# Band scores in row halves, five early gates, and a new order in the even steps of a hybrid attention layer

## The reference, cut to what matters

```python
h  = rms_norm(x, mix_norm)
c_q, c_kv, k_pe, q_s, k_s, v_s = split(h @ w_in)
y_mla = mla_attention(c_q, c_kv, k_pe, ...) @ w_o_mla      # 8 heads, block-causal
y_swa = swa_attention(q_s, k_s, v_s, rel_bias, sinks) @ w_o_swa
g_mla, g_swa = sigmoid(h @ w_gate)                         # 2 x 1024 columns: 16 tiles of 128
x = x + (g_mla * y_mla + g_swa * y_swa) @ w_out

# swa_attention: 8 chunks of 64 queries, 16 query heads, 2 key heads of width 64,
# each chunk sees its own 64 keys and the 64 before it (the "band" of 128 keys)
logits = einsum('bcqhgd,bckhd->bchgqk', q, kb) * 64 ** -0.5 + rel_bias
m = maximum(max(logits), sink)
p = exp(logits - m);  p = p / (sum(p) + exp(sink - m))
o = einsum('bchgqk,bckhd->bcqhgd', p, vb)
```

## Time and profile before

| | |
|---|---|
| median of 3 runs | 1121.86 us (1121.82 to 1121.98) |
| the profiled execution, its own time | 1122.17 us |
| its span | 1120.4 us |
| mean granted TensorE clock | 0.998 |
| busy in the span: PE, DVE, ACT, POOL | 1109.7, 567.0, 419.0, 149.1 us |

### The profile page before, as it was taken

One profiled execution on the slowest core, in us unless ns is written; L12 is line 12 of the kernel. 1 busy time (PEld: TensorE's weight loads), 2 busy tenths in 40 slices (PEclk: granted clock), 3 DMA queues, 4 the chain that ended last, 5 costly groups with the idle time before them and its releaser, 6 DMA issues.

```text
span 1120.4 us, 14760 instructions
## 1 busy us (share of the span) xinstructions
PE 1109.7 (99%) x5194; PEld 908.4 (81%) x5194; DVE 567.0 (51%) x852; ACT 419.0 (37%) x719; POOL 149.1 (13%) x119
## 2 busy tenths in 40 slices
PE   9999999999999999999999999999999999999996
PEld 7888888888888888777777788888888888888896
DVE  6644344433455536876565554546443444434454
ACT  7322222222335325776544533334221233212253
POOL 0211011100114102320000002231110011101122
PEclk9999999999999999999999999999999999999999
DMA  7235222332224221051321232322233222323222
GB/s 269 87 100 122 95 94 94 97 105 98 94 70 132 98 94 61 11 149 50 118 72 62 73 97 94 95 94 94 94 98 105 97 94 94 94 95 103 88 71 76
DMA packets 35262, 107.21 MB, mean 96 GB/s; under 512 B 4224, under 2 KB 7968, under 8 KB 35216
## 3 DMA queue, kind: packets, MB, share of 16 engines
q1 hardware_dynamic: 34464, 105.43, 29.1%
q0 software_dynamic: 192, 0.78, 0.6%
q10 hardware_dynamic: 560, 0.41, 0.1%
HBM read 101.76 MB, written 2.88 MB: 93 GB/s over the span
## 4 chain that ended last, share of the span: by engine, by line
PE 97%; DVE 1%; ACT 1%; issue 0%; POOL 0%; DMA 0%; SPq 0%; DVEq 0%; POOLq 0%; ACTq 0%
PE bank L1352 29%; PE bank L1354 29%; PE bank L1353 29%; PE bank L1502 2%; PE bank L1532 1%; PE bank L1697 1%; PE bank L1699 1%; PE bank L1698 1%; PE bank L1557 1%; PE bank L1492 1%; PE bank L1542 1%; DMA x<-in_x_t 0%; PE bank L1464 0%; PE bank L1459 0%; PE bank L1469 0%
## 5 line engine op out<-in xcount | busy, mean ns | idle before, releaser
L617 ACT ACTIVATE w_hi<-staged 128x1024 fp32r<-128x1024 f32 x182 | 193.0, 1061 | 543.5 <-PE bank L1354 543.4
L1352 PE MATMUL bank<-xg_hi,w_hi 128*128 128x512 f32 x1000 | 395.0, 395 | 0.0
L1354 PE MATMUL bank<-xg_hi,w_lo 128*128 128x512 f32 x1000 | 389.5, 389 | 0.0
L1353 PE MATMUL bank<-xg_lo,w_hi 128*128 128x512 f32 x1000 | 389.3, 389 | 0.0
L922 DVE TENSOR_TENSOR w_lo<-staged,w_hi 128x1024 fp32r<-128x1024 f32 x182 | 225.5, 1239 | 107.9 <-ACT w_hi L617 107.8
L1352 PEld LDWEIGHTS bank<-xg_hi,w_hi 128*128 128x128 f32 x1000 | 187.7, 188 | 44.0 <-issue 6.1
L1354 PEld LDWEIGHTS bank<-xg_hi,w_lo 128*128 128x128 f32 x1000 | 187.7, 188 | 39.8
L1353 PEld LDWEIGHTS bank<-xg_lo,w_hi 128*128 128x128 f32 x1000 | 187.8, 188 | 38.6 <-issue 0.7
L511 POOL TENSOR_TENSOR h_lo<-hid,h_hi 128x512 f32 x44 | 70.6, 1604 | 590.7 <-ACT h_hi L640 534.9
L1352 PE MATMUL bank<-h_hi,w_hi 128*128 128x512 f32 x304 | 118.4, 389 | 0.2 <-POOL h_lo L511 0.2
L1353 PE MATMUL bank<-h_lo,w_hi 128*128 128x512 f32 x304 | 118.3, 389 | 0.0
(11 more groups left out here) (182 smaller groups left out, 1062.6 us busy)
## 6 DMA issues: line engine op xcount, KB each, us to landing
staged<-in_ffn_w SPq DMA_DIRECT2D x118, 512.0 KB, 3.3
staged<-in_w_gate SPq DMA_DIRECT2D x16, 512.0 KB, 3.7
staged<-in_w_in SPq DMA_DIRECT2D x15, 512.0 KB, 3.3
staged<-in_ffn_w SPq DMA_DIRECT2D x16, 384.0 KB, 3.1
staged<-in_w_ob SPq DMA_DIRECT2D x8, 512.0 KB, 3.4
staged<-in_w_out SPq DMA_DIRECT2D x8, 512.0 KB, 3.4
x<-in_x_t SPq DMA_DIRECT2D x8, 256.0 KB, 5.1
staged<-in_w_oa SPq DMA_DIRECT2D x4, 512.0 KB, 3.3
```

Of the source, the lines that this page charges most:

```text
L617: nc.scalar.activation(w_hi[:, u % SPLIT, :], staged[:, u % STAGED, :], ACT.Copy).then_inc(hi_done, 1)
L1352: nc.tensor.matmul(o, wh, hi, start=start, stop=False)
L1353: nc.tensor.matmul(o, wh, lo, start=False, stop=False)
L1354: return nc.tensor.matmul(o, wl, hi, start=False, stop=stop)
```

## The change

Four things are changed together.

1. Band scores. Key heads are no longer laid out with zeros. `band_scores(c)` makes all scores of a chunk at once, as 8 matmuls of 64 rows and 128 columns: those of key head 0 use partitions 0 to 63 and write bank 4, those of key head 1 use partitions 64 to 127 and write bank 5, in turn. Step 2c is now key head 0 of chunk c and step 2c+1 key head 1. TensorE issues the group in even steps only, after the transposes, and it waits for the exponentials of both steps of the chunk before. `swa_values(c)` becomes two matmuls of 512 columns in column halves.
2. Five gates instead of three (`EARLY_GATES`) stand in the band slots, and the slots from 0 to 17 are filled anew. Slots of even number hold two halves of a large product, slots of odd number one, as a rule. In the later slots two gates fewer are spread.
3. Order on the engines. VectorE in an even step: `scores(n+2)`, the split, `scores(n+3)`; in an odd one only the split. ScalarE in an odd step: `exponentials(n+2)` ahead of the split; in an even step as before. GpSimd's fillers come one slot later. The first two scores and exponentials are no longer inside the projection loop.
4. A second copy of the rotary table goes to another tile (`root_sq`), so its DMA now waits for `lat_step` and stands ahead of the load of the `uk` unit; gate slots are numbered 0 to 16.

Diff, cut to its core:

```diff
-EARLY_GATES = 3
+EARLY_GATES = 5
...
-            [("rest", 0, "kv"), ("gate", 0, 0)],
-            [("rest", 4, "q"), ("gate", 0, 1), ("kpe", 0, 1), ("sum", 0, "q"), ("uk", 0, 0)],
-            [("uk", 1, 0), ("uk", 2, 0), ("root", 0, "q")],
-            [("split", 1, "gate"), ("uk", 3, 0), ("uq", 0, 0)],
-            [("uq", 1, 0), ("gate", 1, 0)],
...
+            [("rest", 0, "kv")] + halves("gate", 1),
+            [("kpe", 0, 1), ("uk", 0, 0), ("uk", 1, 0)],
+            [("sum", 0, "q"), ("rest", 4, "q")] + halves("gate", 2),
+            [("uk", 2, 0), ("split", 0, "uq"), ("uk", 3, 0)],
+            [("split", 3, "gate"), ("root", 0, "q"), ("uq", 0, 0), ("gate", 3, 0)],
+            [("uq", 1, 0), ("split", 4, "gate"), ("gate", 3, 1)],
+            halves("gate", 4),
...
-                if w == UNIT_AT["gate", 1]:
-                    sp.wait_ge(lat_ready, 2)
-                    sp.dma_start(lat[:, 0, :], rope_2).then_inc(rope_in, 16)
+                if w == UNIT_AT["uk", 0]:
+                    sp.wait_ge(lat_step, 3)
+                    sp.dma_start(root_sq[:, :], rope_2).then_inc(rope_in, 16)
...
+            exponentials(0)
             exponentials(1)
...
                 read_transposed(n)
+                if n % 2 == 1 and n + 2 < W_STEPS:
+                    exponentials(n + 2)
                 split_next(PLAN[n])
                 if n >= 1:
                     read_output(n - 1)
-                if n + 2 < STEPS:
+                if (n % 2 == 0 or n + 2 >= W_STEPS) and n + 2 < STEPS:
                     exponentials(n + 2)
...
                 if n + 1 < STEPS:
                     normalise(n + 1)
-                if n + 2 < STEPS:
+                if n + 2 < W_STEPS:
+                    if n % 2 == 0:
+                        scores(n + 2)
+                    split_next(PLAN[n])
+                    if n % 2 == 0:
+                        scores(n + 3)
+                elif n + 2 < STEPS:
                     scores(n + 2)
...
+            def band_scores(c):
...
+                else:
+                    pe.wait_ge(exp_done, 2 * c)
+                for pair in range(SG // 2):
+                    for kv in range(SKV):
+                        rows = slice(kv * SD, (kv + 1) * SD)
+                        last = nc.tensor.matmul(bank[S_BANK + kv][:, pair * BAND:(pair + 1) * BAND],
+                                                qs[rows, pair, c, :, :].rearrange("p a b -> p (a b)"),
+                                                ks[rows, c * CHUNK:c * CHUNK + BAND], start=True, stop=True)
...
-                    for j in range(2):
-                        pair = 2 * half + j
-                        last = nc.tensor.matmul(b[:, j * 2 * BAND:(j + 1) * 2 * BAND],
-                                                qs[:, pair, c, :, :].rearrange("p a b -> p (a b)"),
-                                                ks[:, :, c * CHUNK:c * CHUNK + BAND], start=True, stop=True)
...
-                if n + 2 < STEPS:
+                if W_STEPS <= n + 2 < STEPS:
                     scores(n + 2)
                 transposes(n)
+                if n + 2 < W_STEPS and n % 2 == 0:
+                    band_scores(n // 2 + 1)
                 if 2 <= n <= W_STEPS and n % 2 == 0:
-                    swa_values(n - 2)
-                    swa_values(n - 1)
+                    swa_values(n // 2 - 1)
```

More of the change, by code:

```diff
@@ L61 @@
 WARM, WARM_COLS = 5, 256
-EARLY_GATES = 3
-GATE_SLOTS = (2, 5, 4, 0) + tuple(range(6, 16)) + (1, 3)
+EARLY_GATES = 5
+GATE_SLOTS = (2, 5, 16, 4, 0) + tuple(range(6, 16)) + (1,)
 W_STEPS, M_STEPS = NC * 2, MH * TT
@@ L250, in gate_at @@
         def gate_at(t):
-            return gates[:, GATE_SLOTS[t] // 2, GATE_SLOTS[t] % 2, :]
+            return gates[:, GATE_SLOTS[t], :]
         def sum_at(k, low):
-            slot = GATE_SLOTS[2 * k + low]
-            return summed[:, slot // 2, slot % 2, :]
+            return summed[:, GATE_SLOTS[2 * k + low], :]
         def group_bank(n):
@@ L570, in _ @@
             normalise(0)
-            for piece in PLAN[0]:
-                filler(*piece)
             for n in range(STEPS):
@@ L575, in _ @@
                     normalise(n + 1)
-                for piece in PLAN[n + 1]:
+                for piece in PLAN[n]:
                     filler(*piece)
+            for piece in PLAN[STEPS]:
+                filler(*piece)
             pool.wait_ge(*own)
@@ L1110, in scores @@
                 if n < W_STEPS:
-                    c, half = n // 2, n % 2
+                    c, kv = n // 2, n % 2
                     tiles = b[:, :].rearrange("p (t k) -> p t k", t=4)
-                    done(nc.vector.tensor_tensor(b[:, :], b[:, :],
-                                                 bias[:, 2 * half:2 * half + 2].rearrange("p a b c -> p (a b c)"),
-                                                 ALU.add))
+                    done(nc.vector.tensor_tensor(tiles, tiles, bias[:, :, kv, :], ALU.add))
                     if c == 0:
@@ L1245, in _ @@
                     b = bank[(g + U_KS) % 4]
-                    dve.wait_ge(ks_clear, 1)
-                    for h in range(SKV):
-                        rows = slice(h * SD, (h + 1) * SD)
-                        e = nc.vector.tensor_tensor(ks[rows, h, CHUNK:CHUNK + S], b[rows, :], rms[rows, :], ALU.mult)
-                    e.then_inc(grp_read, 1)
+                    nc.vector.tensor_tensor(ks[:, CHUNK:CHUNK + S], b[:, :], rms[:, :], ALU.mult).then_inc(grp_read, 1)
                     dve.wait_ge(grp_ready, g + U_VS + 1)
@@ L1266, in _ @@
                     split_lo(u + w + SPLIT)
+            dve.wait_ge(bias_in, 16 * SG)
+            scores(0)
+            scores(1)
             normalise(0)
-            scores(1)
             for piece in PLAN[0]:
@@ L1505, in _ @@
+                pe.wait_ge(exp_done, n - 1)
+                h, i = m_step(n)
+                if i == 0:
+                    pe.wait_ge(grp_read, g + GROUP_AT["uq", Q_NOPE[h // 2]] + 1)
+                    pe.wait_ge(q_spread[h // 2], 16 * 4)
+                    pe.wait_ge(kpe_spread, 16)
+                nc.tensor.matmul(b[:, 0:query_keys(i)], qm[:, h, norm_rows(i)], km[:, h, 0:query_keys(i)],
+                                 start=True, stop=True).then_inc(s_ready, 1)
             pair_product(u, g, from_x, KD, arrive=(xg_ready, KD))
@@ L1529, in transposes, with swa_values @@
                 for t in range(4 if n < W_STEPS else m_step(n)[1] + 1):
-                    to = (t % 2) * 2 + t // 2 if n < W_STEPS else t
-                    last = nc.tensor.transpose(b[:, to * P:(to + 1) * P], probs[:, n % 2, t * P:(t + 1) * P], idn[:, :])
+                    last = nc.tensor.transpose(b[:, t * P:(t + 1) * P], probs[:, n % 2, t * P:(t + 1) * P], idn[:, :])
                 last.then_inc(t_ready, 1)
-            def swa_values(n):
-                half = n % 2
-                pe.wait_ge(t_read, n + 1)
-                if n >= 2:
-                    pe.wait_ge(o_read, n // 2)
-                for h in range(SKV):
-                    rows = slice(h * SD, (h + 1) * SD)
-                    last = nc.tensor.matmul(bank[O_BANK][rows, half * 2 * P:(half + 1) * 2 * P], vband[:, n // 2, rows],
-                                            probs_t[:, n % 2, h * 2 * P:(h + 1) * 2 * P], start=True, stop=True)
-                last.then_inc(pv_done, 1)
+            def swa_values(c):
+                pe.wait_ge(t_read, 2 * c + 2)
+                if c >= 1:
+                    pe.wait_ge(o_read, c)
+                for kv in range(SKV):
+                    rows = slice(kv * SD, (kv + 1) * SD)
+                    nc.tensor.matmul(bank[O_BANK][rows, :], vband[:, c, rows], probs_t[:, kv, :],
+                                     start=True, stop=True).then_inc(pv_done, 1)
             def mla_values(n):
@@ L1635, in _ @@
             filler(*PLAN[0][0])
-            scores(1)
+            band_scores(0)
             for piece in PLAN[0][1:]:
```

67 lines of the change are left out of this document (25 added, 42 removed).

## The result

The changed kernel takes 1131.55 us (median of 4 runs, 1130.92 to 1132.15), the kernel before in the same rounds 1121.92 (1121.82 to 1122.21). The ratio is 1.0085 with an interval of 1.0068 to 1.0103: slower by 9.6 us. The profiled execution took 1131.85 us with a span of 1130.1 and a mean granted clock of 0.992, for 1122.17, 1120.4 and 0.998 before.

What follows compares the result with a forecast made beforehand. TensorE was taken to bound the kernel, in flight 1109.7 of 1120.4 us. New waits 11.4 less gain 5.3 and old wait 0.5 gave +5.6 on 1122.17; the median 0.3 lower, 1127.5 us; own range 1124 to 1131, whole 1121 to 1132.

Steps and rivals of the forecast that it cites:

- the falling clock: Rival: granted clock falls to 1.2 GHz behind the 3.85 us idle, next gate half takes 5.4 for 2.7: 1130.2 us, chance 0.10.
- serial halves: Rival: row halves of the band scores run one after the other, TensorE has 7.0 us more: 1132.7 us, chance 0.10.
- The walk through the lists: Following each engine's instruction list through the band with timeline durations, to find TensorE's new waits: 11.4 us in sum.
- Row halves: Band scores: both halves run beside each other, 0.87 us a chunk, 8.5 us with mode changes; a gain of 5.3.
- first transposes: Band steps 0 to 5: TensorE waits 0.7 us, as maxima, memsets, reciprocals and scaling take 6.1 behind 5.4 of cover.
- `uk` 0: After step 8's band scores, values and rotary product, TensorE waits 0.8 us for VectorE's two roundings (`lat_ready`).
- sum of squares: After two `uk` products and transposes, TensorE waits 3.85 us for VectorE's rotary read in step 8, which starts late.
- gate 2: Behind the sum of squares, TensorE waits 0.3 us for ScalarE's copies of the first `uk`.
- `uq`: Step 10: the `uq` product waits 2.85 us for ScalarE and then `w_lo` of unit 19.
- gate 3: After the `uq` product, TensorE waits 2.05 us for `w_lo` of unit 20.
- gate 4: Step 12: after `uq`, the gate's second half and transposes, TensorE waits 0.85 us for `w_lo` of unit 21.
- The first rival: Waits stay at their least or below, VectorE not late at step 8: 6.3 us of waits, 1122.4 us; chance 0.25.

Runs made afterwards that it cites:

- kept_busy: Changed kernel with throw-away TensorE matmuls, four ahead of the sum of squares in step 9 and three ahead of the first `uq` product in step 11: 1129.71 us.
- kept_busy_too: kept_busy with three more dummy matmuls between `uq` 0 and gate 3: 1128.27 us, ratio 1.0052.
- before_wait: Kernel before, with eight more VectorE multiplications inside its read of the rotary product, to make TensorE wait: 1126.81 us, ratio 1.0040.
- relieved: new_plan with the `uk` unit's split by itself in slot 8 and the query norm's sum of squares moved behind `uk` 1: 1119.47 us, ratio 0.9979.
- after_early_split: Changed kernel with the `uk` unit's split by itself in slot 8, behind the low parts of the latents: 1131.21 us, ratio 1.0080.
- rotary_early: Changed kernel with the rotary key's second product one slot earlier, ahead of gate 1: 1130.94 us, ratio 1.0075.
- split_first: Changed kernel with the even steps' split ahead of reading the transposes on ScalarE and ahead of both sets of maxima on VectorE: 1134.03 us, ratio 1.0107.
- new_plan: Changed kernel with slots 8 to 15 filled anew; row halves, five early gates and VectorE and ScalarE order kept: 1126.33 us, ratio 1.0036.
- old_plan: Changed kernel's new code with the plan and three early gates of the kernel before: 1132.23 us, ratio 1.0100.

## Why the prediction was right in direction and 4 us too low

The forecast was 1127.5 us, with a range of its own from 1124 to 1131, and 1131.55 was measured: over that range, and inside the whole one of 1121 to 1132 by 0.45 us. Two rivals lay on the slow side, the falling clock at 1130.2 and serial halves at 1132.7. The walk through the lists held, the clock was left out.

- *Row halves.* They overlap, gain 4.85 us for 5.3. The group costs 1.09 us for the 0.87 + 0.175 of the forecast: 8 pairs at 0.112 are 0.89, the first pair stands 0.10 longer and the way to the values costs 0.09. The Trainium skill (TensorEngine Tiling (Array Packing), "Gotcha 1: PSUM Pressure") wants row tiles to write separate banks; with banks 4 and 5 the trace has the overlap, and no run here tries one bank.
- *Waits by place,* predicted and measured: first transposes 0.7, 0.48; `uk` 0 0.8, 0.38; sum of squares 3.85, 3.85; gate 2 0.3, 0.1; `uq` 2.85, 2.82; gate 3 2.05, 1.24; gate 4 0.85, 0.69. All seven are where the lists put them; six stand in the view of waits with the predicted releasers, and gate 2's is a distance only. The first transposes, `uk` 0 and gate 2 came out at a third to two thirds of their forecast. The walk is right in its inner times too: from the end of the band scores of step 6 (468.76) it had VectorE start step 8 at 14.25 and end the rotary read at 20.65, and the trace has 14.14 and 20.75. Gate 3 is short only because `uq` ran at half clock; at the full clock of kept_busy it waits 2.04.
- *The first rival* (waits at their least or below): excluded, 9.6 us for its 6.3. *Serial halves:* excluded, 1.09 us a group.
- *The clock.* This is the term that failed. The prediction had "the clock falls" as a rival with 0.10 and left the term out of the forecast. Its ground, that the clock stood at 1.00 through a wait of 0.5 us, was called no test in the same sentence; with waits of 3.85 and 2.85 us in the forecast, the term belonged in it. The rival's price, 2.7 us for one half of a gate, was also half of what came, since the clock fell twice. 1127.5 - 1.8 (waits smaller) + 0.45 (gain smaller) - 0.15 (the old wait was 0.67, not 0.5) + 5.4 = 1131.4, for 1131.55 measured. Without the half clock the same kernel stands 5.9 us over the one before (kept_busy_too), and the forecast was 5.6; they lie this close partly by luck, since smaller waits and a smaller gain cancel in it. The Trainium skill (TensorE: Matmul & The Clock Gate, "HAM oscillation") speaks of idle gaps between bursts of work; kept_busy, kept_busy_too and before_wait agree with it in direction, for single gaps in an otherwise full stream. Not every gap did it in these runs (last section).
- *Later steps:* as before, with their empty slots, as predicted.
- *What the forecast did not see,* because no term of it rests on it: several late engines stand behind one another here. Where the sum of squares is moved, ScalarE's copies come up with 2.9 us, which the forecast had as 0.3. It was right as a sum and would have misled as a list of what each wait is worth.

## What to carry to other kernels

Where TensorE sets the end, a forecast of new waits of microseconds is incomplete without the clock behind them: in this kernel 9.6 us of waits brought 5.4 us of half clock. It is no fixed price for a wait: waits of 2.5 and 2.8 us had no half clock right behind them in two other runs, and one of 1.4 us had a stretch that cost some 1.7. Read, at a long wait, what else is late behind the one that is named, since removing that one brings the next (2.9 us of 3.85 here), and follow the chain back to an idle stretch of the late engine: here VectorE waited 3.95 us with ready work queued behind the waiting instruction. A change that costs 0.85% held a gain of 0.42%, and the difference between the two was where some ten entries of a table and two copies stand.

## What the runs showed of the hardware

- A wait as short as 1.4 us (relieved, 1.24 of it shown as idle) was followed by 3.41 us at a granted clock of 0.50; the one in the band of the kernel before (0.67, 0.5 as idle) was not. Waits of 2.99 (before_wait), 3.07 (after_early_split), about 3.1 (rotary_early) and 2.04 (kept_busy) were followed by 3.41 us, 3.85 by 6.83. The 2.82 of `uq` was followed by 6.83 too, with the 1.24 of gate 3 inside it.
- The length of a wait alone does not decide. In split_first the same `uq` wait of 2.82 us was followed by 5.1 us at the full clock, and half clock (3.41 us, from 514.53) came only behind gate 3's of 2.03. In new_plan the full clock stood through a wait of 2.45 us and another of 2.97 right behind it, and 3.41 us of half clock came 1.1 us after the second. In old_plan no half clock followed an idle time of 1.68 us at 491. What decides stays open. Windows behind the first of the two waits, split_first and then new_plan:

```profile
509.50:513.50 4.00, 2.26 (x9) 1.51 (x9) 1.24 (x3) 2.81 (x11) 1.04 (x1) 1.00 0.01 4
490.50:494.80 4.30, 1.57 (x6) 0.95 (x6) 0.91 (x3) 4.23 (x15) 1.04 (x1) 1.00 0.98 257
```

- Ten dummy matmuls in three waits kept the granted clock at 1.00 and made the kernel 3.3 us faster (kept_busy_too).
- Row halves of float32 matmuls that write two banks start 7 ns apart if issued in turn (1.09 us a group), and for the most part one after the other, 0.112 us apart, if not (1.64 us).
- In relieved, VectorE's `nmax`, 128x4, took 1.22 us at 483.50, where it takes 0.16 elsewhere (487.71 in the changed kernel); new_plan has the same at 486.23 (1.20 us, beside the same addition from 486.13). GpSimd's addition beside it ran from 483.40 to 484.69:

```profile
483.40 1.29 POOL L566 TENSOR_TENSOR km<-km,rot 64x512 f32<-64x512 f32 x1
```

The small instruction ended as the large one of the other engine did (484.72); which resource they share, no run here tells apart.
